# Forgetting attention of 16 heads: woven with its query and gate projections, its bias rows and causal mask added in PSUM by TensorE

## What is computed

```python
def fox_mixer(h, w_qg, w_out, k, v, c):          # 16 heads of 64, 512 queries, 512 keys
    proj = h @ w_qg
    q, g = jnp.split(proj, [D_MODEL], axis=-1)
    q = q.reshape(B, S, H, DH) * (DH ** -0.5)
    ...
        logits = jnp.einsum('bqhd,bkhd->bhqk', qi, k).astype(jnp.float32)
        logits = logits + (ci[..., :, None] - c[..., None, :])
        logits = jnp.where(mask, logits, -jnp.inf)
        p = jax.nn.softmax(logits, axis=-1)
        ...
    o = o * jax.nn.sigmoid(g)
    return o @ w_out
```

## Time and profile before

| | |
|---|---|
| median of 3 runs | 2994.97 us (2994.58 to 2995.88) |
| the profiled execution | 2995.05 us |
| its span, first to last instruction | 2993.1 us |
| mean granted TensorE clock | 0.945 of full |
| busy, share of the span | PE 94%, DVE 53%, ACT 35%, POOL 3% |

### The profile page before, as it was taken

How to read it: one execution, slowest core, us unless ns; L and a number is a source line. 1 busy time by engine, 2 the same in 40 slices (tenths; PEclk the granted TensorE clock), 3 DMA queues, 4 the chain that set the end, 5 groups by cost and what they waited for, 6 DMA issues and landing times. The chain is left out here.

```text
span 2993.1 us, 31051 instructions
## 1 busy us (share of the span) xinstructions
PE 2814.0 (94%) x12266; PEld 2153.5 (72%) x12266; DVE 1589.6 (53%) x2652; ACT 1051.4 (35%) x1606; POOL 97.8 (3%) x121
## 2 busy tenths in 40 slices
PE   6999999999998889999999978899999999899998
PEld 4887688877874346888878843478888765588886
DVE  4455767674234654746563255446664499444333
ACT  3344534242233444433345233332223311432222
POOL 0000000100000000000000000001110010000000
PEclk9999999997997899999998968799999999999999
DMA  4423244541221002332333300026663211123231
GB/s 130 119 77 100 74 138 147 176 134 41 88 88 39 1 15 71 99 96 88 91 100 102 98 22 1 0 85 197 193 194 106 64 50 56 57 85 98 94 98 50
DMA packets 282503, 266.28 MB, mean 89 GB/s; under 512 B 13217, under 2 KB 268471, under 8 KB 282103
## 3 DMA queue, kind: packets, MB, share of 16 engines
q1 hardware_dynamic: 266759, 210.47, 22.9%
q0 software_dynamic: 14560, 53.78, 6.2%
q10 hardware_dynamic: 1040, 0.07, 0.0%
HBM read 262.17 MB, written 2.10 MB: 88 GB/s over the span
## 5 line engine op out<-in xcount | busy, mean ns | idle before, releaser
L451 DVE TENSOR_TENSOR w_lo<-raw,w_hi 128x1024 fp32r<-128x1024 f32 x396 | 484.7, 1228 | 895.0 <-ACT w_hi L446 894.1
L446 ACT ACTIVATE w_hi<-raw 128x1024 fp32r<-128x1024 f32 x396 | 418.0, 1057 | 1156.1 <-PE G L1787 1019.3
L1787 PE MATMUL G<-H_hi,w_hi 128*128 128x512 f32 (+1 forms) x1984 | 793.7, 400 | 23.5 <-DVE H_lo L337 7.9
L1787 PE MATMUL G<-H_lo,w_hi 128*128 128x512 f32 (+1 forms) x1984 | 776.6, 391 | 0.0
L1787 PE MATMUL G<-H_hi,w_lo 128*128 128x512 f32 (+1 forms) x1984 | 776.5, 391 | 0.0
L1787 PEld LDWEIGHTS G<-H_hi,w_hi 128*128 128x128 f32 x1984 | 378.0, 191 | 116.4 <-issue 36.4
L1787 PEld LDWEIGHTS G<-H_lo,w_hi 128*128 128x128 f32 x1984 | 378.1, 191 | 84.2 <-issue 7.7
L1787 PEld LDWEIGHTS G<-H_hi,w_lo 128*128 128x128 f32 x1984 | 377.5, 190 | 78.7
L1787 PE MATMUL G<-hid_hi,w_hi 128*128 128x512 f32 x864 | 342.5, 396 | 4.7 <-DVE hid_lo L556 4.7
L1787 PE MATMUL G<-hid_hi,w_lo 128*128 128x512 f32 x864 | 338.2, 391 | 0.0
L1787 PE MATMUL G<-hid_lo,w_hi 128*128 128x512 f32 x864 | 338.1, 391 | 0.0
(11 more groups left out here) (279 smaller groups left out, 2812.9 us busy)
## 6 DMA issues: line engine op xcount, KB each, us to landing
raw<-in_w_ff SPq DMA_DIRECT2D x128, 512.0 KB
mod_w<-in_w_mod POOLq DMA_DIRECT2D x96, 512.0 KB, 4.6
raw<-in_ffn_w_up SPq DMA_DIRECT2D x176, 256.0 KB
raw<-in_ffn_w_down SPq DMA_DIRECT2D x40, 512.0 KB
raw<-in_w_in SPq DMA_DIRECT2D x28, 512.0 KB
raw<-in_mlstm_w_in SPq DMA_DIRECT2D x24, 512.0 KB
raw<-in_kv_w SPq DMA_DIRECT2D x16, 512.0 KB
raw<-in_fox_w_qg SPq DMA_DIRECT2D x16, 512.0 KB
```

Source lines behind the costliest of these rows:

```text
L446: act.activation(w_hi[:, j, :], raw[:, j, :], ACT.Copy).then_inc(hi_done, 1)
L451: dve.tensor_tensor(w_lo[:, j, :], raw[:, j, :], w_hi[:, j, :], ALU.subtract).then_inc(lo_done, 1)
L1787: mm = pe.matmul(G[:, 2 * p + m, 0:n], lw[:, k, ms], rh[:, t, 0:n], start=(t == 0 and q == 0), stop=(t == st["ktiles"] - 1 and q == 2), sk ...
```

## The change

It does three things to the fox attention.

1. The stages `x_q` and `x_g` are cut into eight stages of one group each, in the order q0, g0, q1, g1, ...; q0 and the first half chunk of g0 run ahead of the attention, the rest in 26 units of 12 matmuls, two per head, between the attention's products of heads 0 to 12. Three units of `x_out` run in heads 14 and 15. The splits and evacuations of these stages go into the lists of ACT and DVE at given places (`evacuated_by`).
2. `-c` is written once as two float32r rows (`x_row`, high and low part). For each block PE adds them to the scores in PSUM (two products of 16 rows, L1248), and adds the mask to the diagonal block by a product with the identity (L1250). DVE takes a plain maximum (L1450) and its negative (L1451); ACT exponentiates from PSUM (L1361). The spread row, its copies and the pair copies are gone; keys, queries and values are read in place.
3. The chain that makes `c` and the refill "pre1" are written between the splits of `kv_k`, where they stood behind `x_g` and behind `kv_k`. The transposed blocks have one PSUM bank in place of two; the score banks are two in place of four.

```diff
+        def fox_pe(pe, linear, linear_units, from_h, squares_behind):
+            def scores(h, b):
+                n, hs = 4 * h + b, slice(HP * (h % 2), HP * (h % 2) + HP)
...
+                if n >= 2:
+                    pe.wait_ge(fx["e"], n - 1)
+                logit = M[:, b % 2, 0:(b + 1) * P]
+                pe.matmul(logit, xQ[hs, h // 2, b * P:b * P + P], xK[hs, h // 2, 0:(b + 1) * P], start=True,
+                          stop=False, skip_group_check=True)
+                for part in range(2):
+                    pe.matmul(logit, sel_x[:, h:h + 1].to_broadcast([16, P]), x_row[:, part, 0:(b + 1) * P],
+                              start=False, stop=False, skip_group_check=True)
+                pe.matmul(M[:, b % 2, b * P:b * P + P], x_ident[:], x_mask[:], start=False, stop=True,
+                          skip_group_check=True).then_inc(fx["s"], 1)
...
+            for h in range(FOX_HEADS):
+                for b in range(TB):
+                    if b < 3:
+                        scores(h, b + 1)
+                    elif h < FOX_HEADS - 1:
+                        scores(h + 1, 0)
+                    if b % 2 == 0 and h < 13:
+                        next(work)
+                    if (h, b) in ((14, 2), (15, 0), (15, 2)):
+                        next(outs)
+                    if b == 3:
+                        turn(h, 0)
+                        if h:
+                            values(h - 1)
+                    elif h:
+                        turn(h - 1, b + 1)
...
         def fox_act(act):
...
+            for h in range(FOX_HEADS):
+                for b in range(TB):
+                    exps(h, b)
+                    if b == 3:
+                        turned(h, 0)
+                    elif h:
+                        turned(h - 1, b + 1)
+                    for _ in range(evacuated_by(h, b - 2, 3) - taken):
+                        next(work)
+                        taken += 1
...
         def fox_dve(dve, link):
...
+            for h in range(FOX_HEADS):
+                for b in range(TB):
+                    largest(h, b)
+                    if b >= 2:
+                        scaled(h, b - 2)
+                    elif h:
+                        scaled(h - 1, b + 2)
+                    if b == 0 and h >= 2:
+                        output(h - 2)
+                    for _ in range(evacuated_by(h, b - 2, 2) - taken):
+                        next(work)
+                        taken += 1
```

More of the change, by code:

```diff
@@ L95, in linear_plan @@
     ffn1(0)
-    stages.extend([("kv_v", 4, 8), ("kv_k", 4, 8), ("x_q", 4, 8), ("x_g", 4, 8), ("x_out", 4, 8)])
+    stages.extend([("kv_v", 4, 8), ("kv_k", 4, 8)] + [(name, 1, 8) for name in FOX_STAGES] + [("x_out", 4, 8)])
     ffn1(1)
@@ L1225, in soft_dve, with units_by @@
             skewed(c["pairs"], body, tail)
[L1228 to L1234, removed]
-        def fox_act(act):
+        def units_by(h, b):
+            return 2 + sum(1 for k in range(26) if (k // 2, 2 * (k % 2)) <= (h, b)) if (h, b) >= (0, 0) else 2
@@ new lines, in fox_act @@
+            for _ in range(3):
+                next(keys)
+            act.wait_ge(row_c, 3)
+            act.activation(x_row[:, 0, :], rows[0:16, 4, :], ACT.Copy, scale=-1.0).then_inc(row_c, 1)
+            for _ in range(3):
+                next(keys)
+            act.wait_ge(chunk_used, used_after("kv_k") - 1)
+            for t in range(KC):
+                high(t)
+            next(keys)
+            act.wait_ge(chunk_used, used_after("kv_k"))
+            for t in range(KC, DT):
+                high(t)
@@ new lines, in fox_dve @@
+            next(lows)
+            dve.wait_ge(row_c, 4)
+            dve.scalar_tensor_tensor(x_row[:, 1, :], rows[0:16, 4, :], -1.0, x_row[:, 0, :], ALU.mult,
+                                     ALU.subtract).then_inc(row_c, 1)
+            next(lows)
+            next(lows)
+            for t in range(KC):
+                produce(t)
+            for t in range(KC):
+                low(t)
+                produce(t + KC)
+            next(lows)
+            for t in range(KC, DT):
+                low(t)
@@ L1278, in second_loads @@
+            finish(work)
+            last = FOX_HEADS - 1
+            output(last - 1)
+            scaled(last, 2)
+            scaled(last, 3)
+            mixed(6)
+            output(last)
+            mixed(7)
         def second_loads(sp, load_stage, cols, pairs):
@@ L1923, in _ @@
                 gate_rows(1, 16, t)
-            linear("kv_k", H_hi, H_lo, need=from_h("kv"))
-            linear("x_q", H_hi, H_lo, need=from_h("pre1"))
-            linear("x_g", H_hi, H_lo, need=from_h("pre1"))
-            fox_pe(pe)
-            linear("x_out", H_hi, H_lo, need=from_h("fox"), behind=squares_behind("post1"))
+            fox_pe(pe, linear, linear_units, from_h, squares_behind)
             ffn1(1)
```

205 lines of the change are left out of this document (155 added, 50 removed).

## The result

The changed kernel takes **3029.57 us** (median of 4 runs, 3027.59 to 3031.48), the kernel before 2994.77 beside it. The ratio is 1.0116, with a 95% interval of 1.0099 to 1.0134: **slower by 35 us**, where I had forecast 2993 and a range that ended at 3012.

What follows compares the result with a forecast made beforehand. In the attention no engine was full: PE, DVE and ACT waited for each other and PE's clock fell. Terms 151.2 + 32.2 + 6.3 + 1.0 + 6.6 = 197.3 us against 199.4 gave 2993 us, range 2960 to 3012.

Steps and rivals of the forecast that it cites:

- the clock: Woven attention: four waits of 3.6 us lose 1.65 each to half clock, 6.6 us; the twelve of 2 lose nothing.
- the row of 1.79 in the mLSTM: Dense mLSTM before the change: a 1.79 us wait left full clock, taken as evidence that 2 us waits cost no clock.
- the clock falls at every wait: Rival, woven attention: each of twelve 2 us waits costs 1.65 more, 20 us in all, giving 3013 us; chance 18%.
- PE's products: Attention, per head: 6.69 us for scores, transposes and values plus 2.76 for bias and mask; 151.2 us for 16 heads.
- The least of 0.11 for a 128-wide pass: Bias and mask products: by the skill's load time, a 128-wide pass can't be cheaper than 0.11 us, supporting 0.12.
- with each 128-wide pass at 0.21: Upper bound on bias and mask products: 3.3 us a head in place of 2.76, 9 us more in all.
- The new wait: PE ahead of block 3's scores: 1.97 us in heads 1 to 12, more in 1, 5, 9; 3.6 in 13; sum 32.2.
- Tail, start and what was hidden: Attention's ends: tail with slow x_out start 6.3 us, start before head 0 1.0; refill's 6.5 us and gate chain hidden.
- Table loads: Rival, ACT in four heads: loads take about 2.7 us, not 1.28; waits grow 11 us, giving 3004 us; chance 5%.
- The wait isn't there: Rival, woven attention: no new wait ahead of block 3's scores; without 32.2 and 6.6 us, 2954 us; chance 17%.
- The refill gap: Between kv_k and q0: the refill is interleaved with kv_k and q0, so its 6.5 us go.

Runs made afterwards that it cites:

- e1_shift: Changed kernel with ScalarE's and VectorE's share of a woven weight chunk one step later in their lists, TensorE's order unchanged: 2973.6 us, ratio 0.9922.
- e6_two: e1_shift plus two unread 128x1024 copies by ScalarE ahead of block 1's exponential in heads 1 to 12: 3006.1 us, 1.0029.
- e9: e1_shift with half units behind every block's scores, one unit more ahead of the loop, chunk work and evacuations placed later in the lists: 2975.6 us, 0.9941.
- e13_waits_one_pass: Changed kernel, lists and waits as they are, with one bias pass of 128 rows in place of two of 16: 3001.8 us, 1.0020.
- e11_one_pass: e1_shift with high and low bias rows in one zero-padded tile of 128 rows, one pass per block in place of two: 2945.6 us, 0.9832.
- e10_unwoven_no_rows: e3_unwoven without bias and mask products, forget bias and causal mask left out of the result: 2931.4 us, 0.9791.
- e4: e1_shift without bias and mask products, forget bias and causal mask left out of the result: 2932.6 us, 0.9792.
- e3_unwoven: Changed kernel's products, but the eight projections all stand ahead of the attention: 3009.9 us, 1.0049.
- e15_two_full: e3_unwoven with bias rows padded with zeros to 128 rows, still two passes per block: 2956.3 us, 0.9866.
- e2_low_only: Changed kernel with only VectorE's list changed, the low part one step later, behind block 1's maximum: 3005.0 us, 1.0031.

## Why the prediction was wrong

The step that failed is **the clock**: "So the four waits of 3.6 cost 4 x 1.65 = 6.6, the twelve of 2 nothing." By the starts of the heads, less their waits and the same heads of e1_shift at full clock, eight heads with a wait of 1.81 lose 3.2 us each and head 2 loses 1.6, head 1 loses 4.1, and heads 5 and 9 lose 2.9 and 3.0: 37 us. With (13.5 - 3.28) / 2 = 5.1 for head 13, whose window of 13.5 us at half clock holds its wait, that is 42 us, 36 more than the term.

I had taken the row of 1.79 in the mLSTM as the rule for a wait of that length. It was no rule: e6_two shows the clock fall in every head at 0.97, e9 shows it stay at 0.93. Length alone doesn't decide. What the runs show in place of the nothing: waits of 2.2 and 4.0 us cost 27 us of clock even among products that fill 64 or 128 rows (e13_waits_one_pass against e11_one_pass), and the passes of 16 rows, an operation for which the trace before had no clock to show, add about 12. Why the same sort of wait left the clock full in the mLSTM stays open.

The rival "the clock falls at every wait" had the right mechanism and half of the price: 1.65 a head was taken from 3.3 us at half clock, and the stretches are 6.8. Its 3013 is 17 us short.

**The other steps:**
- *PE's products.* 15.02 less two units of 2.72 (10.88 / 4) is 9.58 a head, where 9.45 was predicted: 2 us in all. Unwoven it is 9.44. Without bias and mask a head is 7.00 (e10_unwoven_no_rows, 7.27 from 961.43 to 968.70, less a wait of 0.27), where 6.69 was predicted, so bias and mask are 2.44, where 2.76 was: the two errors cancel, which is luck. That e4 comes out at 41 as well is in part luck, since the clock comes back there and new waits come up. The least of 0.11 for a 128-wide pass, by which the prediction supported its 0.12, does not hold here: between passes of 128 rows it is 0.06 (953.22 to 953.28), near the 56 ns that it names beside it. The bound "with each 128-wide pass at 0.21" wasn't touched. The term was right in sum, and what it left out, that these passes act on the clock of all others, is what e3, e10 and e15 show.
- *The new wait.* 30.5 us in 13 places, 32.2 predicted; 1.81 for 1.97, 3.65 for 3.67, 3.28 for 3.6. e1_shift and e2_low_only show that its cause is the one named, the split and DVE's low part ahead of block 1's maximum and exponential.
- *Tail, start and what was hidden.* 197.3 as predicted, plus 2 of products, less 2 of waits, plus 36 of clock is 233; measured are 232.3, so these terms were off by 1 in sum. One by one they aren't shown: 3.4 us at half clock ahead of the first wait (852.3 to 855.7) stand in none of them. The refill gap is gone as said.
- *Table loads.* Each is 1.28 us again, so that rival is out. The Trainium skill, ScalarE: Activation LUTs, "What ACT_TABLE_LOAD costs", makes up its 2.7 us of about 1.28 for the load and 1.38 for a drain. The load agrees; of a drain these rows show nothing: in head 5 a load starts at 944.36 and the sigmoid at 945.65, the second load at 946.69 and the exponential at 947.99.
- *The wait isn't there*, 2954: e1_shift is the version without it, and takes 2973.6. The other 20 are in its windows: 7 us lost to the clock from 970 to 1050 (80 x 0.09), 10 from 1050 to 1090 (40 x 0.26), and the three waits of 4.1.

**The change in its parts.** Bias and mask in the bank, unwoven, with the gate chain and the refill moved: +15 us against before (e3_unwoven, 3009.9). Weaving, with the lists as they stand: another 20 (3029.6). Weaving with the lists one step later: 36 less than unwoven (2973.6). And the bias in rows of 128: 28 less again, **2945.6 us for e11_one_pass, 50 us (1.7%) faster than before**, which is the version to keep. Once rows and lists are right, weaving is worth 4 us (2949.4 unwoven), which these runs don't tell from nothing.

What stays open: whether it is the 16 rows or the changes of rows around them that bring the clock down, why the 64 rows of the scores don't, why the unwoven attention starts with 20 to 27 us at half clock in every version, and how long a wait may be; the runs give points, no law.

## What to carry to other kernels

When a wait is put into PE's stream, price it twice: by its length, and by the clock behind it. Take the second price from a wait that has the same kind of products around it; a dense stretch elsewhere in the program is no witness. Where an engine's list is shared, ask of each shift what the very next item is needed for: one step later was worth 56 us here and cost nothing, 26 of them waits and 30 clock. And fill up passes that use few rows of the array, with zeros if need be, before judging an order of work by them.

## What the hardware showed beside

- Two passes per block of 16 rows kept the granted clock at 0.69 while PE was recorded busy for 150 of 150 us; the same two with zeros to 128 rows left it at 1.00 from 944 us on (e3_unwoven, e15_two_full). The Trainium skill, TensorE: Matmul & The Clock Gate, "Part 1: The HAM clock gate", has the gate follow how busy TensorE has been. By the recorded busy time these two are alike; so it is not that busy time alone which it follows, and the measurement decides.
- The same products are found at either level: in e15_two_full PE is recorded busy for 22.00 of 22.00 us at 0.50 behind the first wait, and for 125.31 of 126.00 at 1.00 later. With the first wait of the unwoven attention came 20 us (e10_unwoven_no_rows) to 27 us (e3_unwoven) at half clock, with one of 3.9 us late in e11_one_pass 6.8.
- Padding cost no time either: in e15_two_full two passes of 128 rows and 384 keys take 0.45 us to the start of the mask, where two of 16 rows take 0.53 in the changed kernel (903.74 to 904.27), and the mask itself is only 0.06 us ahead of the next product.

```profile
960.53 0.61 PE L1248 MATMUL M<-x_row,sel_x 128*128 128x384 f32 x2
960.98 0.22 PE L1250 MATMUL M<-x_mask,x_ident 128*128 128x128 f32 x1
961.04 0.50 PE L1259 MATMUL M<-ident,xL 128*128 128x128 f32 x3
```

- A pass of 128 columns in float32r, the mask, starts 0.06 us ahead of the next product where it stands behind a pass of 128 rows (e11_one_pass), half of what I took for it, and 0.16 where it stands behind one of 16 (e1_shift).
